# Second key and query pair of the mixer: rotary halves in buffers of their own, rope before the stacks; window blocks of values read back in two halves

## The reference, cut to what matters

```python
u = rmsnorm(h, mix_pre_g[l])
qa, ka, va, qb, kb, vb, qc, kc, vc, gl = split(u @ w_in[l])
oa = neighbourhood_attention(qa, ka, va, na_rpb[l])          # A: 8 heads, windows of 8 rows x 16 columns
ob = sliding_window_attention(rope(qb), rope(kb), vb, sink)  # B: 8 query heads, 2 key heads, |i-j| <= 128
oc = differential_attention(rope(qc), rope(kc), vc, ...)     # C: 4 pairs of heads of width 64, dense
yb = einsum('bsnc,ncd->bsnd', stack([oa, ob, oc]), w_branch[l])
merged = sum(sigmoid(gl + b_gate[l]) * yb, over the branches)
h = h + rmsnorm(merged @ w_out[l], mix_post_g[l])
```

## Time and profile before

| what | us |
|---|---|
| median of 3 timed runs | 3592.2 |
| lowest and highest | 3590.93, 3592.7 |
| the profiled execution's own time | 3585.11 |
| its span in the trace | 3583.3 |

### The profile page before, as it was taken

One profiled execution on the slowest core, in us unless ns is written; L12 is line 12 of the kernel. 1 busy time (PEld: TensorE's weight loads), 2 busy tenths in 40 slices (PEclk: granted clock), 3 DMA queues, 4 the chain that ended last, 5 costly groups with the idle time before them and its releaser, 6 DMA issues.

```text
span 3583.3 us, 42774 instructions
## 1 busy us (share of the span) xinstructions
PE 3462.6 (97%) x17080; PEld 2879.5 (80%) x17080; DVE 1789.0 (50%) x3164; ACT 1372.9 (38%) x2437; POOL 346.5 (10%) x327
## 2 busy tenths in 40 slices
PE   8999899999999999999899999999999889999998
PEld 7888787878888888888787877888888777878887
DVE  5442565755544345432666564644257655544432
ACT  4222353634432233222454543522246354233221
POOL 0110110021011001100111021011000001201100
PEclk9999999999999999999999999999999999999999
DMA  3223332253232323232423262222331311323232
GB/s 139 97 92 92 102 100 78 70 141 94 75 101 96 91 84 102 96 91 91 109 74 94 76 144 79 95 95 94 95 96 64 93 56 63 105 86 100 94 93 72
DMA packets 110871, 332.23 MB, mean 93 GB/s; under 512 B 18248, under 2 KB 19016, under 8 KB 110672
## 3 DMA queue, kind: packets, MB, share of 16 engines
q1 hardware_dynamic: 98352, 306.82, 27.8%
q0 software_dynamic: 12320, 22.66, 3.1%
HBM read 306.23 MB, written 4.21 MB: 87 GB/s over the span
## 4 chain that ended last, share of the span: by engine, by line
PE 91%; DVE 4%; ACT 2%; DMA 2%; issue 1%; POOL 0%; SPq 0%; DVEq 0%; ACTq 0%; POOLq 0%
PE PS L696 89%; PE PS L1018 1%; ACT wh L1137 1%; DMA PT<-val_d 1%; DVE wl L1609 1%; DVE stk L1889 0%; DMA raw<-in_gu 0%; DMA raw<-in_win 0%; ACT stk L1137 0%; DMA tmp<-tmp 0%; DVE tmp L1917 0%; DMA stk<-stk 0%; DVE tmp L1938 0%; ACT tmp L1137 0%; DVE small L1923 0%
## 5 line engine op out<-in xcount | busy, mean ns | idle before, releaser
L696 PE MATMUL PS<-uh,wh 128*128 128x512 f32 (+1 forms) x3336 | 1267.0, 380 | 31.5 <-DVE ul L1637 14.6
L696 PE MATMUL PS<-uh,wl 128*128 128x512 f32 (+1 forms) x3336 | 1261.9, 378 | 0.0
L696 PE MATMUL PS<-ul,wh 128*128 128x512 f32 (+1 forms) x3336 | 1255.9, 376 | 0.0
L1609 DVE TENSOR_TENSOR wl<-raw,wh 128x1024 fp32r<-128x1024 f32 (+2 forms) x595 | 709.5, 1194 | 903.8 <-ACT wh L1137 901.6
L1137 ACT ACTIVATE wh<-raw 128x1024 fp32r<-128x1024 f32 (+2 forms) x595 | 583.8, 984 | 559.7 <-PE PS L696 545.9
L696 PEld LDWEIGHTS PS<-uh,wh 128*128 128x128 f32 x3336 | 630.5, 189 | 159.2 <-DVE tmp L2019 10.3
L696 PEld LDWEIGHTS PS<-ul,wh 128*128 128x128 f32 x3336 | 630.6, 189 | 119.9
L696 PEld LDWEIGHTS PS<-uh,wl 128*128 128x128 f32 x3336 | 629.9, 189 | 116.8 <-issue 1.4
L696 PE MATMUL PS<-gh,wh 128*128 128x512 f32 (+1 forms) x968 | 363.6, 376 | 0.0
L696 PE MATMUL PS<-gh,wl 128*128 128x512 f32 (+1 forms) x968 | 362.1, 374 | 0.0
L696 PE MATMUL PS<-gl,wh 128*128 128x512 f32 (+1 forms) x968 | 359.6, 372 | 0.0
(11 more groups left out here) (215 smaller groups left out, 3334.2 us busy)
## 6 DMA issues: line engine op xcount, KB each, us to landing
raw<-in_gu SPq DMA_DIRECT2D x220, 512.0 KB, 3.4
raw<-in_win SPq DMA_DIRECT2D x139, 512.0 KB, 3.5
raw<-in_dn SPq DMA_DIRECT2D x80, 512.0 KB, 3.5
raw<-in_wbr SPq DMA_DIRECT2D x72, 256.0 KB, 2.6
raw<-in_dn SPq DMA_DIRECT2D x40, 384.0 KB, 3.1
raw<-in_wout SPq DMA_DIRECT2D x24, 512.0 KB, 3.5
raw<-in_wv SPq DMA_DIRECT2D x20, 512.0 KB, 3.4
stk<-stk SPq DMA_DIRECT2D x72, 128.0 KB, 2.4
```

Source lines behind the costliest of these rows:

```text
L696: return e.matmul(out, lhs, rhs, start=start, stop=stop, skip_group_check=True)
L1609: tt(wl[:, p % 4, 0:n], raw[:, p % 3, 0:n], wh[:, p % 4, 0:n], SUB).then_inc(*S.lo.up(("lo", p)))
```

## The change

The turn buffers become four: `tmp[5]` for the first q and all later tags, `tmp[2]` for the first key, `rb[1]` for q1, `gates[0]` for k1, each with a semaphore of its own. DVE does rope q1 directly behind the gate's evacuation and rope k1 behind one piece of `ahead`, both before the first `stack`. `values` on TensorE asks for each bank just ahead of its first matmul. The window blocks are laid out anew, j = 1 and 2 in V[1..4], j = 3 and 4 in PT[1], PT[2], V[0], PT[0]; the first four are asked for after merge m = 0, the last four after m = 3, and each half has its own semaphore. On ACT, in the steps past the last unit, `turned` comes before `ahead`, the tanh and the stacks.

```diff
@@ window_values
-            return V[:, i, :] if i < 5 else PT[:, i - 5, :]
+            return V[:, i + 1, :] if i < 4 else [PT[:, 1, :], PT[:, 2, :], V[:, 0, :], PT[:, 0, :]][i - 4]
@@ turn_of
-            return 2 if tag[0] == "k" and tag[2:] in (("C", 0), ("C", 1)) else 5
+            return {("q", "C", 1): 2, ("k", "C", 0): 1, ("k", "C", 1): 3}.get((tag[0], *tag[2:]), 0)
+
+        def turn_at(i):
+            return [tmp[:, 5, :], tmp[:, 2, :], rb[:, 1, :], gates[:, 0, :]][i]
@@ semaphores
-            vi = Signal(ctx.enter_context(nc.semaphore("s_windows")))
-            rp = [Signal(ctx.enter_context(nc.semaphore(f"s_rope{i}"))) for i in range(2)]
+            vi = [Signal(ctx.enter_context(nc.semaphore(f"s_windows{i}"))) for i in range(2)]
+            rp = [Signal(ctx.enter_context(nc.semaphore(f"s_rope{i}"))) for i in range(4)]
@@ tensor: values
-                for j in tiles(v):
-                    take(vb[j], S.aa, "vv", v, st, j)
                 for kc in range(4):
                     p = JOBS["v", v, st, kc].first
                     E.wait_ge(S.lo, "lo", p)
                     for j in tiles(v):
+                        if kc == 0:
+                            take(vb[j], S.aa, "vv", v, st, j)
@@ tensor: weighted
-                    E.wait_ge(S.vi, "windows", v)
+                    E.wait_ge(S.vi[(j - 1) // 2], "windows", v)
@@ scalar: attention
+                    u = n - A.lag
+                    if n >= A.n and u < A.n:
+                        turned(v, st, u)
                     ahead(fill_reach(fill, n))
...
-                    u = n - A.lag
-                    if 0 <= u < A.n:
+                    if 0 <= u and n < A.n:
                         turned(v, st, u)
@@ vector: rope
-                for dst, table in ((temp_of(tag), cos), (turn, sin)):
-                    if dst == turn and turn in turned:
-                        E.wait_ge(S.rp[turn == 2], "roped", turned[turn])
+                for dst, table in ((tmp[:, temp_of(tag), xs], cos), (turn_at(turn)[:, xs], sin)):
+                    if table is sin and turn in turned:
+                        E.wait_ge(S.rp[turn], "roped", turned[turn])
@@ vector: mixer
                 evacuate(JOBS["g", v, 2, 0], v)
+                rope(JOBS[q1], v)
                 ahead(reach(JOBS[q1]))
+                rope(JOBS[k1], v)
                 ahead(reach(JOBS[k1]))
                 stack(q)
-                rope(JOBS[q1], v)
                 stack(k)
                 ahead(reach(JOBS["v", v, "C", 0]))
-                rope(JOBS[k1], v)
                 ahead(reach(JOBS["v", v, "C", 1]))
                 stack(q1)
@@ gpsimd: windows_in, mixer
-            def windows_in(v):
+            def windows_in(v, part):
                 E.wait_ge(S.vw, "values", v)
-                E.wait_ge(S.pl, "macc", v, 1, 3, 0)
-                for j in range(1, 5):
+                if part:
+                    E.wait_ge(S.pl, "macc", v, 1, 3, 0)
+                for j in (2 * part + 1, 2 * part + 2):
...
-                    if m == 3:
-                        windows_in(v)
+                    if m in (0, 3):
+                        windows_in(v, m // 3)
```

More of the change, by code:

```diff
@@ L658, in build @@
             vw = Signal(ctx.enter_context(nc.semaphore("s_values_out")))
-            vi = Signal(ctx.enter_context(nc.semaphore("s_windows")))
-            rp = [Signal(ctx.enter_context(nc.semaphore(f"s_rope{i}"))) for i in range(2)]
+            vi = [Signal(ctx.enter_context(nc.semaphore(f"s_windows{i}"))) for i in range(2)]
+            rp = [Signal(ctx.enter_context(nc.semaphore(f"s_rope{i}"))) for i in range(4)]
             kd = [Signal(ctx.enter_context(nc.semaphore(f"s_k_halves{i}"))) for i in range(2)]
         signals = [S.mm, S.sc, S.tp, S.pv, S.st, S.hi, S.aa, S.ex, S.pt, S.an, S.lo, S.dv, S.sx, S.dn, S.pl, S.par,
-                   S.id, S.on, S.lv, S.mt, S.rv, *S.raw, *S.x, *S.o, *S.tab, *S.tb, *S.rp, *S.kd, S.vw, S.vi]
+                   S.id, S.on, S.lv, S.mt, S.rv, *S.raw, *S.x, *S.o, *S.tab, *S.tb, *S.rp, *S.kd, S.vw, *S.vi]
         def freed(job, c):
@@ L1309, in stack @@
                 if st in "CB":
-                    E.wait_ge(S.rp[turn_of(tag) == 2], "roped", tag)
+                    E.wait_ge(S.rp[turn_of(tag)], "roped", tag)
                 E.wait_ge(*stack_guard(v, st, which, p))
@@ L1866, in rope @@
                 E.wait_ge(S.mm, "job", tag, 0)
-                for dst, table in ((temp_of(tag), cos), (turn, sin)):
-                    if dst == turn and turn in turned:
-                        E.wait_ge(S.rp[turn == 2], "roped", turned[turn])
+                for dst, table in ((tmp[:, temp_of(tag), xs], cos), (turn_at(turn)[:, xs], sin)):
+                    if table is sin and turn in turned:
+                        E.wait_ge(S.rp[turn], "roped", turned[turn])
                     if which == "q":
-                        i = stt(tmp[:, dst, xs], ps, 0.125, table[:, :], MUL, MUL)
+                        i = stt(dst, ps, 0.125, table[:, :], MUL, MUL)
                     else:
-                        i = tt(tmp[:, dst, xs], ps, table[:, :], MUL)
+                        i = tt(dst, ps, table[:, :], MUL)
                 i.then_inc(*S.dv.up(("ev", tag, 0)))
@@ L2332, in rotate @@
                 for a, o in ((32, 0), (0, 32), (96, 64), (64, 96)):
-                    e.dma_start(tmp[o:o + 32, temp_of(tag), X0:TW], tmp[a:a + 32, turn_of(tag), X0:TW], accum_op=ADD).then_inc(
-                        *S.rp[turn_of(tag) == 2].land(("roped", tag)))
+                    e.dma_start(tmp[o:o + 32, temp_of(tag), X0:TW], turn_at(turn_of(tag))[a:a + 32, X0:TW], accum_op=ADD).then_inc(
+                        *S.rp[turn_of(tag)].land(("roped", tag)))
             def merge(v, n, m, first):
@@ L2355, in values_out @@
                     e.dma_start(VAL[P * (j - 1):P * j, :], V[:, j, :]).then_inc(*S.vw.land(("values", v)))
-            def windows_in(v):
+            def windows_in(v, part):
                 E.wait_ge(S.vw, "values", v)
-                E.wait_ge(S.pl, "macc", v, 1, 3, 0)
-                for j in range(1, 5):
+                if part:
+                    E.wait_ge(S.pl, "macc", v, 1, 3, 0)
+                for j in (2 * part + 1, 2 * part + 2):
                     for r in range(2):
                         src = bass.AP(VAL.tensor, (256 * r + window(j)[1]) * 512, [[64 * 512, 4], [512, 32], [1, 512]])
-                        e.dma_start(window_values(j, r), src).then_inc(*S.vi.land(("windows", v)))
+                        e.dma_start(window_values(j, r), src).then_inc(*S.vi[part].land(("windows", v)))
             def mixer(v):
```

## The result

| | before | after |
|---|---|---|
| median of the timed runs, us | 3591.56 (3588.01 to 3592.7, 4 runs) | 3564.76 (3561.46 to 3567.51, 4 runs) |
| the profiled execution's own time | 3585.11 | 3567.51 |
| its span in the trace | 3583.3 | 3565.7 |

The ratio of the times is 0.9927, 95% interval 0.9909 to 0.9944: 26.8 us faster by the medians. The forecast was 3556.2 with a range of 3551 to 3570.

A forecast was written before the change was run, and what follows sets the result against it. The prediction took TensorE, busy 97% of the span, to bound the kernel; 25.3 + 10 + 0.3 = 35.6, say 36 us, takes the timed median of 3592.2 to 3556.2, range 3551 to 3570.

The forecast's parts named there:

- Part 1: Start of both mixers: second pair's ropes in front and banks asked tile by tile end TensorE's wait; 25.3 us saved.
- the 2.1 that I called the narrowest: Values of C: second value piece ready at 422.9, wanted at 425.0; claimed as the smallest slack, 2.1 us.
- rival B: Start: VectorE holds off GpSimd's issues, the fourth value piece comes 2.4 us late, about 4 per mixer; 3564, chance 0.09.
- The rule of the Trainium skill weighed in the forecast: Start: GpSimd's DMA issue is blocked until VectorE's operation ends, 620 ns becoming some 3100; could delay the first rotations.
- Part 2: Attention of A: window blocks read back in two halves, so both window waits go; 10 us saved, bounds 3 to 11.2.
- At 216 GB/s, 1 MB is 4.9 us less backlog: Before A: four early window blocks leave a full DMA stretch for one 0.53 busy, relieving the former by 4.9 us.
- weight loads there landing under 9 us: Attention of A: sign that the forecast is right, with no wait on a window block.
- rival A: Attention of A: key halves or weights are late by as much as the windows were; 3564, chance 0.13.
- Rival C: Branch stage: the early 1 MB slows weight loads, 2.8 us lost per piece; slower kernel, 3612, chance 0.02.
- Part 3: The rest: `turned` before `ahead` in steps past the last unit, acting in S; 0.3 us saved, bounds -1 to 0.7.
- the window term: Attention of A: the 10 us saving forecast for asking for the window blocks in two halves.
- the likeliest case: Whole kernel: the forecast itself without rivals, spanning 30 to 39 us saved, 3553 to 3562; chance 0.72.

The follow-up runs named there:

- E5: The changed kernel with the window part undone: old layout, all eight blocks after m = 3, one wait for all; 3564.3 us, ratio 0.9931.
- E4: The changed kernel with the first four window blocks asked for after m = 3, the last four after m = 7; 3553.9 us, 3552.6 when run again.
- E1: The changed kernel with all eight window blocks asked for after m = 3, new layout and two semaphores kept; 3563.6 us, ratio 0.9931.
- E9: The changed kernel with only the two blocks of j = 1 asked for after m = 0, the other six after m = 3; 3559.2 us, ratio 0.9923.
- E3: The changed kernel with only two of the eight window blocks read back, after m = 3, so A's sum is wrong; 3556.5 us, ratio 0.991.

## Why the forecast was right, and the step that failed

**Part 1 was right, in mechanism and size.** The steps: bank 3 free 1.9 us after the gate's evacuation started at 421.32 (forecast 1.9); no wait in the values; clock 1.00; attention of C 13.3 us sooner (forecast 13). Predicted 25.3 us, measured 25.5 in the trace, 23.3 for the part alone by medians (E5). The narrow place was the fourth value piece: its subtraction ended at 435.8 where it was wanted at some 437.5, 1.7 us of slack where my sum gave it 3.2 (436.0 less 432.8; the 2.1 that I called the narrowest was the second piece's). It came later because the first key's stack did (433.20), which waited for the rotation to land. Of rival B nothing is seen: GpSimd's first eight issues took 6.57 us beside eight VectorE operations, against 6.55 before, 0.82 each; its sixteen went from 420.52 to 433.44, 0.81 each. The rule of the Trainium skill weighed in the forecast (SBUF — State Buffer, "A bandwidth-pool intuition that's wrong") did not show in DMA issue here; the page's own case is a `tensor_copy` of VectorE, and none of the operations beside the issue was one, a condition that I had left out.

**Part 2 failed.** The step is "At 216 GB/s, 1 MB is 4.9 us less backlog", with the sign "weight loads there landing under 9 us": the first landed after 11.0. I saw a stretch with a DMA share of 0.53 and took it for free room, and asked what the early megabyte takes away from A, not what it meets. It meets the load of A's first piece, issued at 739.92, 1.4 us behind GpSimd's first block. That load took until 750.91; ACT stood for it, each later piece and buffer followed late, and the remaining loads fell into the second half's burst. The pile of work that ACT and VectorE then caught up with shows as TensorE's waits for VectorE in units 6 to 8 of the first mixer and unit 3 of the second. For the latter the chain can be read: a load is late, ACT's conversion waits for it, VectorE's subtraction for the conversion, and the scores' operation on VectorE stands behind the subtraction until just before TensorE goes on at 2071.15:

```profile
2068.44 1.06 ACT L1140 ACTIVATE wh<-raw 128x1024 fp32r<-128x1024 f32 x1 [2.31 <-DMA raw<-in_win]
```

```profile
2069.53 1.23 DVE L1614 TENSOR_TENSOR wl<-raw,wh 128x1024 fp32r<-128x1024 f32 x1 [4.04 <-ACT wh L1140]
2070.67 0.42 DVE L1943 CUSTOM_DVE_ANT_0 tmp<-PS,tb 128x256 f32<-128x256 f32 x1
```

All window and key waits went, as forecast, and the time did not: 1.7 us of 10 measured. That is rival A in its form "the weights are late", with a price even below the 3 us that I gave it. Rival C's slow loads are there too, one stage later than I had put them: not in the branch products but in A's first pieces. TensorE halted for none of them; the delay reached it through VectorE. The sign "weight loads there landing under 9 us" was a poor one besides: E4, the fastest kernel, has one of 9.5 us and E1 one of 13.4.

E1, E9 and the changed kernel show the dose, E3 that with a quarter of the traffic the waits for weights are gone, and E4 that the same bytes at a later moment (its two halves are asked for 8.4 us before A's first score and 2.6 behind it, the changed kernel's 16.4 and 8.0 before) shorten A by 7 us and save 7 to 8.5 more by the medians. That VectorE's catching up is what turns late weights into TensorE's waits is read from the timeline, and was not tested by itself.

The Trainium skill, DMA: Bandwidth & Descriptors, section "SWDGE vs HWDGE vs iDMA", says that transfers issued by GpSimd and by SyncE stand in different queues of the same DMA engines, which take them in turn. By equal turns, my estimate from that rule and the measured rate, a load of 0.5 MB would be through once 1 MB had moved, 4.8 us at 220 GB/s; the trace agrees that the load is held back by blocks of another queue, and its 11.0 us are over twice that. The measurement decides; why the turns were not equal is open.

**Part 3** was priced at 0.3 us with bounds from -1: by the trace it is -0.3 (2.47 us of idle time for 2.18). The wait before the values of F stayed, 2.98 us for 2.89, as said.

**The sum.** 25.5 + 1.7 - 0.3 = 26.9, against 35.6. Of the 8.7 us that are missing 8.3 are the window term; the forecast, 3556.2, and the median, 3564.8, are 8.6 apart. So the likeliest case, 3553 to 3562, did not come true: what came is rival A, to which I had given 0.13, and its 3564. The range held because its upper part was drawn from that rival and from B.

## What to carry to other kernels

A low DMA share is no free room: before moving a transfer into a gap, list which loads are issued in the microseconds around it and who needs them first, and price the move by what those lose. Spread the blocks so that they lie between two deadlines; here after the fourth and the eighth merge, not the first and the fourth. Splitting one wait into two semaphores did more for A than the earlier start of the transfer (56.4 us in E1 against 62.7 in E5; by the medians, 2.3 us, that is no more than a hint), and a reordering on one engine (the ropes) may need its partner on another (asking for a bank only when it is written) to pay in full.

## What the hardware showed beside that

Where the early issues made two merges fall together on GpSimd, a VectorE subtraction of 0.69 us took 2.37. GpSimd and VectorE, changed kernel:

```profile
741.24 1.31 POOL L2348 TENSOR_TENSOR macc<-macc,gates 128x512 f32<-128x512 f32 x1
742.50 1.29 POOL L2348 TENSOR_TENSOR macc<-macc,gate_v 128x512 f32<-128x512 f32 x1
```

```profile
739.20 0.69 DVE L1614 TENSOR_TENSOR wl<-raw,wh 128x512 fp32r<-128x512 f32 x1
741.98 2.37 DVE L1614 TENSOR_TENSOR wl<-raw,wh 128x512 fp32r<-128x512 f32 x1
```

In the second mixer it is 2.12. The merges themselves took 1.3 each there, where one took 1.81 in the kernel before. That difference is the other side of the same coin. In the kernel before, a merge starts just behind a subtraction on VectorE, and then the subtraction keeps its 0.69 and the merge takes the longer time:

```profile
746.23 1.79 POOL L2343 TENSOR_TENSOR macc<-macc,gates 128x512 f32<-128x512 f32 x1 [0.98 <-DVE gates L2019]
```

```profile
746.18 0.69 DVE L1609 TENSOR_TENSOR wl<-raw,wh 128x512 fp32r<-128x512 f32 x1
```

Each time the one that started while the other was running took longer. The same section of the Trainium skill's page SBUF — State Buffer says that GpSimd and a VectorE operation on both of its ports exclude each other, one waiting for the other; for these elementwise operations the 2.37 us agree with it, while DMA issue beside VectorE (0.81 each) shows nothing of it.
